# Two gate units moved between the steps of a state-space scan, and their sigmoids behind it

## The reference

```
proj = h @ w_in[i]
q, k, v, z, xbc, dt_raw, gates = split_cols(proj, IN_SPLITS)
...
attn_out = gqa_attention(q, k, v) @ w_attn_proj[i]
ssd_y = ssd_branch(z, xbc, dt_raw, ...)
ssd_out = ssd_y @ w_ssd_proj[i]
g_attn, g_ssd = jnp.split(jax.nn.sigmoid(gates), N_BRANCH, axis=-1)
mixed = (g_attn * attn_out + g_ssd * ssd_out) @ w_out[i]
...
def ssd_chunked(xs, dt, a, bm, cm):
    y_diag = jnp.einsum("bcgls,bcgrls,bcsgrp->bclgrp", cb, decay_in, xd)
    states = jnp.einsum("bclgn,bcgrl,bclgrp->bcgrpn", bc, decay_states, xd)
    def step(h, inp):
        st, dec = inp
        return h * dec[..., None, None] + st, h
    _, prev = lax.scan(step, h0, (states, chunk_decay))
    y_off = jnp.einsum("bclgn,bcgrpn,bcgrl->bclgrp", cc, prev, jnp.exp(a_cs))
    return y_diag + y_off
```

## Time and profile before

| | us |
|---|---|
| median of 3 runs | 2368.75 |
| lowest, highest | 2365.58, 2369.27 |
| the profiled execution | 2360.32 |
| its span, first to last instruction | 2358.5 |

### The profile page before, as it was taken

One profiled execution on the slowest core, in us unless ns is written; L12 is line 12 of the kernel. 1 busy time (PEld: TensorE's weight loads), 2 busy tenths in 40 slices (PEclk: granted clock), 3 DMA queues, 4 the chain that ended last, 5 costly groups with the idle time before them and its releaser, 6 DMA issues.

```text
span 2358.5 us, 28203 instructions
## 1 busy us (share of the span) xinstructions
PE 2202.5 (93%) x10837; PEld 1825.0 (77%) x10848; DVE 1143.1 (48%) x1836; ACT 1007.5 (43%) x2029; POOL 959.9 (41%) x730
## 2 busy tenths in 40 slices
PE   7999899999988997899999997897899999999997
PEld 6788778888877776778888876775597887888886
DVE  3445565554345666465553364564535335544322
ACT  5666444443235564254442256455344234323222
POOL 3555554343456752453443433123423334322232
PEclk9999999999989999899999998898999999999998
DMA  4112122322213221123223211110012221232221
GB/s 156 54 54 72 51 93 90 107 90 99 98 61 110 81 68 34 60 72 106 91 94 109 92 65 36 37 37 19 19 46 91 97 107 72 90 106 91 101 98 52
DMA packets 29846, 183.08 MB, mean 78 GB/s; under 512 B 3984, under 2 KB 4112, under 8 KB 11920
## 3 DMA queue, kind: packets, MB, share of 16 engines
q1 hardware_dynamic: 29712, 181.27, 22.2%
HBM read 174.97 MB, written 2.10 MB: 75 GB/s over the span
## 4 chain that ended last, share of the span: by engine, by line
PE 82%; DVE 7%; ACT 5%; issue 3%; POOL 2%; DMA 0%; SPq 0%; POOLq 0%; ACTq 0%; DVEq 0%
PE PS L1423 80%; PE PS L1548 1%; POOL LO L2702 1%; DVE bQS L2160 1%; DVE cCVT L2585 0%; PE PS L1661 0%; DMA RAW<-wall 0%; ACT HI L1750 0%; DVE aQS L2160 0%; POOL bTQ L2760 0%; DVE cST L2566 0%; POOL bROT L2755 0%; DVE YH L2262 0%; DVE XL L2237 0%; DVE T_f L2232 0%
## 5 line engine op out<-in xcount | busy, mean ns | idle before, releaser
L2702 POOL TENSOR_TENSOR LO<-RAW,HI 128x512 fp32r<-128x512 f32 (+2 forms) x382 | 540.7, 1432 | 623.9 <-ACT HI L1750 623.6
L1423 PE MATMUL PS<-XH,HI 128*128 128x512 f32 (+1 forms) x1584 | 640.4, 404 | 34.1 <-ACT cCU L2067 10.4
L1423 PE MATMUL PS<-XH,LO 128*128 128x512 f32 (+1 forms) x1584 | 626.0, 395 | 0.0
L1423 PE MATMUL PS<-XL,HI 128*128 128x512 f32 (+1 forms) x1584 | 619.7, 396 | 1.4 <-DVE XL L2237 1.4
L1750 ACT ACTIVATE HI<-RAW 128x512 fp32r<-128x512 f32 (+3 forms) x668 | 365.7, 608 | 171.3 <-PE PS L1423 168.0
L2160 DVE TENSOR_TENSOR LO<-RAW,HI 128x512 fp32r<-128x512 f32 (+2 forms) x286 | 304.5, 1069 | 248.3 <-ACT HI L1750 248.0
L1423 PEld LDWEIGHTS PS<-XH,HI 128*128 128x128 f32 (+1 forms) x1584 | 302.9, 191 | 98.0 <-issue 21.0
L1423 PEld LDWEIGHTS PS<-XH,LO 128*128 128x128 f32 (+1 forms) x1584 | 302.1, 191 | 66.0 <-issue 1.1
L1423 PEld LDWEIGHTS PS<-XL,HI 128*128 128x128 f32 (+1 forms) x1584 | 301.7, 191 | 63.9 <-DVE XL L2237 3.3
L1423 PE MATMUL PS<-HH,HI 128*128 128x512 f32 x528 | 205.4, 389 | 0.0
L1423 PE MATMUL PS<-HL,HI 128*128 128x512 f32 x528 | 205.4, 389 | 0.0
(11 more groups left out here) (397 smaller groups left out, 3355.7 us busy)
## 6 DMA issues: line engine op xcount, KB each, us to landing
RAW<-wall SPq DMA_DIRECT2D x138, 1024.0 KB, 4.8
RAW<-wall SPq DMA_DIRECT2D x24, 896.0 KB, 4.4
bROT<-bTQ SPq DMA_DIRECT2D x64, 64.0 KB, 2.0
RAW<-wall SPq DMA_DIRECT2D x5, 512.0 KB, 3.3
XF<-xT SPq DMA_DIRECT2D x4, 512.0 KB, 5.3
outT<-XR SPq DMA_DIRECT2D x8, 256.0 KB, 2.0
FP<-cfp SPq DMA_DIRECT2D x1, 1024.0 KB, 6.8
MKF<-cmask SPq DMA_DIRECT2D x1, 704.0 KB, 11.0
```

Of the source, the lines that this page charges most:

```text
L1423: return e.matmul(out, a, b, start=start, stop=stop)
L2702: return e.tensor_tensor(out, x, h.bitcast(F32), ALU.subtract)
```

## The change

The two gate units of quarter 0, `cga` 0 and `cgs` 0, are taken between the last `cx` unit and the first `cz` unit. `opening()` and `scans()` are chained into one generator that runs beside their 32 k-steps at 1.6 steps each, together with what is left of the chores; the `cz` units get the old rate of 0.36. The evacuation of a gate tile becomes a step of its own, `mgp`. The scaled products of quarter 0 wait in a new tile `GA0` and in `CTH`, and their four sigmoids stand behind `yn`; quarter 0 mixes in `CU` in place of `SG`. The heads keep banks 2 and 3, the states take bank 4 + g for both directions, since the gate tiles need banks 0 and 1. In `scans` each state step now ends with a `yield`. In the mix, the order for quarter 0 becomes `cpa` 0, `cga` 1, the eight `yt`, `cps` 0; quarter 1 begins with `cpa` 1.

```
-RATES = (0.37, 0.18, 1.0, 0.36, 1.0, 0.9, 0.9)
+RATES = (0.37, 0.18, 1.0, 1.6, 1.0, 0.9, 0.9, 0.36)
...
+    out += [("cq", 0), ("ck", 0), ("cq", 1), ("cv", 0)] + [("cx", j // 2) for j in CONV[::2]] + [("cga", 0), ("cgs", 0)]
+    out += [("cz", i) for i in range(4)] + [("cpa", 0), ("cga", 1), ("cps", 0)]
+    for i in range(1, 4):
+        out += [("cga", i)] * (i > 1) + [("cpa", i), ("cgs", i), ("cps", i)]
...
-                    at_bank(("sh", h, dr), 2 + dr + 2 * (h % 2))
+                    at_bank(("sh", h, dr), 2 + dr)
...
-                        b, s = pick(), ("so", dr, idx, g)
+                        b, s = 4 + g, ("so", dr, idx, g)
...
-                        b, s = pick(), ("sp", dr, idx, g)
+                        b, s = 4 + g, ("sp", dr, idx, g)
...
                 for i in range(PACE):
-                    next(left[(PACE * n + i) % 2], None)
+                    if next(left[(PACE * n + i) % 2], finished) is not finished:
+                        yield
...
-        first = opening()
-        while chores or together_chores:
-            chore()
-            next(first, None)
-        for _ in first:
-            pass
-        alongside(scans(), RATES[3])
+        def gate(kind, i, later=False):
+            for j, t in enumerate(lin_fm((kind, i), "X", evac=lambda j, t: product(kind, i, j, t))):
+                if not later:
+                    put("m" + kind[1:], i, j)
+
+        def product(kind, i, j, t):
+            freed[tiles[t].bank] = ("mgr", put("mgp", "m" + kind[1:], i, j, t))
+
+        alongside(itertools.chain(opening(), scans()), RATES[3])
+        gate("cga", 0, True)
+        gate("cgs", 0, True)
         until(lambda: sdone[0] >= 4 and all(finished))
+        beside[1] = RATES[7]
...
+        for kind in ("mga", "mgs"):
+            for j in range(2):
+                put(kind, 0, j)
+        shares(0)
+        gate("cga", 1)
         for j in range(8):
             b, s = pick(), ("yt", j)
...
+        mix(0)
+        for i in range(1, 4):
+            if i > 1:
+                gate("cga", i)
+            shares(i)
+            gate("cgs", i)
+            mix(i)
...
+    GA0 = sb("cGA0", 1024, F32, E0 + 32 * K)
...
+            return blk(GA0 if kind == "mga" else CTH, j)
...
-            elif kind in ("mga", "mgs"):
-                i, j, t = a
-                x = 1024 * j + (512 if kind == "mgs" else 0)
+            elif kind == "mgp":
+                gk, i, j, t = a
                 e.wait_ge(*when_(ag.tiles[t].full))
-                if i > 0:
+                if i > 1:
                     e.wait_ge(*when("mxl", *whole["mps", i - 1, j]))
-                e.tensor_tensor(SG[:, x:x + 512], PS[ag.tiles[t].bank][:, :], RPS[:, :], ALU.mult).then_inc(SEM["mgr"], 1)
+                elif i == 0 and gk == "mgs":
+                    e.wait_ge(*when("cxm", "cxm", CONV[-1]))
+                elif i == 0:
+                    e.wait_ge(*when("turn", "tu", 3))
+                e.tensor_tensor(gated(gk, i, j), PS[ag.tiles[t].bank][:, :], RPS[:, :], ALU.mult).then_inc(SEM["mgr"], 1)
```

53 lines of the change are left out of this document (25 added, 28 removed).

## The result

The changed kernel takes 2378.54 us (median of 5 runs, 2375.28 to 2384.01), the kernel before 2365.58 in the same comparison; the ratio is 1.0056, with a 95% interval from 1.0041 to 1.0071. It is slower by about 13 us. The forecast was +7.5 us, 2376.3, in a range of 2365 to 2385; it started from 2368.75, the median of three runs that was known then.

What follows compares the result with a forecast made beforehand. TensorE, busy for 93% of the span, was taken as the bound, so time could come only from its waits or half clock. Scan +13.2 and mix -5.7 gave +7.5 on 2368.75, so 2376.3 us, range 2365.0 to 2385.0.

Steps and rivals of the forecast that it cites:

- the forecast's own case: Whole kernel: slower by +4.7 to +12 us, around the +7.5 forecast; chance 0.45.
- The mix: From last `cz` matmul to `cpa` 1: gives back only 5.7 us, with new waits of 7.3 and 8.9 us.
- The scan: Scan with both gates moved in: 84.4 us instead of 71.2, +13.2, as 15.4 us stay above 69.0 of work.
- the start: Scan's beginning: TensorE at half clock until 1620, 3.4 us lost (bounds 1.5 and 6).
- the bursts: Two state runs `sp so so sp so so` in the scan: waits on VectorE's chain, 7.0 us together (bounds 5.0 and 8.5).
- the copy on ScalarE behind the eight `y0`: Scan: backward `sp` shares the forward one's bank and waits for this copy, 1.8 us (bounds 0 and 3).
- small waits: Scan's opening and between states: 0.2, 0.6, 0.5 and 0.3, in sum 1.6 us; last `cxt` among them.
- falls of the clock: Scan: one fall to half clock after a wait, 1.6 us (bounds 0 and four falls, 6.4).
- The new banks: Scan: heads on two banks and states sharing one per group, priced as waits at some 3 us.
- The clock's rule: Skill page: only a long idle gap costs the clock; by it the change comes out 1.6 us better; not followed.
- The fast one: Rival: the clock holds and waits shrink, scan +5.4, mix gives 10.5, together -5.1, 2363.7 us; chance 0.08.
- The convoy: Rival: gate steps and scan steps delay each other, ScalarE may bound, nothing hidden, +16.1, 2384.9 us; chance 0.17.

Runs made afterwards that it cites:

- e1_cover: Changed kernel with the mix reordered: `cga` 1 ahead of `cpa` 0 and `cgs` 1 ahead of `cps` 0, scan untouched; 2362.43 us, ratio 0.9990 to the kernel before.
- e11_defer: e7_toggle with one more convolution piece issued per opening piece, the last convolution's transposition `cxt` 7 kept at its old place on TensorE; 2357.56 us.
- e2_block: Changed kernel with both gate units in one block behind the scan instead of between its steps; 2398.7 us, ratio 1.0144 to the kernel before.
- e3_banks: Kernel before with only the new banks, heads on 2 and 3, states on 4 + g, no gate moved; ratio 1.0090, runs 2372.49 to 2393.27 us.
- e5_states: Kernel before with only a state's product put in the bank of its group, heads keeping four banks, no gate moved; 2386.07 us, ratio 1.0071.
- e6_heads: Kernel before with only the heads put on banks 2 and 3, states in turn as before, no gate moved; 2367.19 us, ratio 1.0002.
- e7_toggle: e1_cover with the states' products and outputs taking banks 4 and 5 in turn instead of by group; 2361.64 us, ratio 0.9979 to the kernel before.
- e12_gaps2: e11_defer with late gate k-steps put into the bursts' waits, one kept between the last head's broadcasts and its output; 2353.56 us, ratio 0.9946 to before.

## Why the prediction was right or wrong

- **The sign and the range.** Right: slower, +13 where +7.5 was forecast; 2378.5 lies within 2365 to 2385. It lies above the forecast's own case (+4.7 to +12) by 1 us. That 2378.5 is only 2 us from 2376.3 is in part luck: the forecast was added to 2368.75, and the kernel before took 2365.58 in the comparison. The change was 5.5 us larger than forecast.
- **The `cz` stretch, nothing.** Right: 74.1 against 74.0.
- **The mix, -5.7.** Right: -6.6, and by the mechanism named. The wait ahead of `cga` 1 was 6.8 (7.3 forecast), `cps` 0 ran step by step, and `cpa` 1 stood 51 us behind the last `cz`. The parts were off and made up for each other: the waits are 12.3 and not 16.2, the clock's loss 8.7 (7.3 without what falls into the long wait) and not 4.8. A chain that VectorE and ScalarE pace ends when it ends, and slow matmuls within it only fill its waits. e1_cover shows that this loss of cover is worth 16 us.
- **The scan, +13.2.** Mis-sized by 6: +19.2. Term by term, forecast and measured: the start 3.4 and 3.4; the bursts 7.0 and 7.1; the copy on ScalarE behind the eight `y0` 1.8 and nothing (it ended at 1658.79 and the product that needs it stands at 1658.84, after gate k-steps at half clock, which covered it); small waits 1.6 and 4.4, of which `cxt` 7 alone has 3.8 where I wrote 0.5, and the last head's output 0.6 where I wrote nothing; falls of the clock 1.6 and about 4.7, one of which, 2.6, is the fall behind `cxt` 7; and 1.8 without a name. So the step that failed is the last `cxt` in the list of small waits. I followed TensorE's list, costed VectorE and ScalarE by their free shares, and did not walk their queues: on ScalarE the convolution's first piece stands behind exponentials and `y0`, and on VectorE its other pieces stand behind a head's product that waits for ScalarE. e11_defer takes away the wait, and some 3 to 4 us with it.
- **The hidden part.** I said that 8.6 of the 21.8 us would be hidden; against the kernel before it was 2.6. The scan of 90.4 also passes my own mark, over 90, at which the gates were to hide nothing. Yet they do much: against the same banks without them in the scan they save 20 us (e2_block). I thought of cover for waits, and the waits stayed at 11.5; what they gave was clock, 8.1 lost instead of 13.5.
- **"The gates keep TensorE denser, so I take one fall."** The number was wrong (two large falls), the thought was right and larger than I made it: with the same banks and no gates the kernel takes 2391 (e3_banks, though one of its four runs took 2372), with the gates' work in a block 2399 (e2_block), and with the gates between the steps 2379.
- **The new banks.** I priced them at some 3 us, as waits. Without gates the states' pairing costs 6 to 24 (e5_states) and the heads' two banks nothing (e6_heads). With the gates in place, going back to banks in turn gives 1 to 3, which the intervals don't tell from nothing (e7_toggle), so in the changed kernel the price was not far off, by luck: the k-steps cover it.
- **The clock's rule.** After 0.87, 2.09 and 0.87 of waits in one burst four matmuls take 3.46 instead of 1.95. The Trainium skill, "TensorE: Matmul & The Clock Gate", section "HAM oscillation — how this bites in real kernels", has only a long gap cost the clock; the trace disagrees here as it did before.
- **The rivals.** The fast one is out: half clock at the start lasted 7.6 us and the mix lost its clock. The convoy (+16.1) came nearer than I allowed, to within 3 us. Its own mark was over 20 us of waits and half clock: what stands above the 69.0 of work is 21.4, of which 19.6 have a name. Of its place I had half. ScalarE, which I named, was late with the first piece of the last convolution, but it was not the bound behind it: there VectorE's queue was, and ScalarE stood idle for 4.18 ahead of the piece that it makes near the end:

```profile
1650.69 0.63 ACT L2106 ACTIVATE cCTH<-cCVT 128x512 f32<-128x512 f32 x1 [4.18 <-DVE cCVT L2609]
```

What stays open: why the clock comes back in one execution of e3_banks and e5_states and not in another, which part of e11_defer's gain is ScalarE's order and which VectorE's, which part of e12_gaps2's last 4 us is the last head's wait, and whether the first wait of 0.69 alone keeps the clock down in the kernels with paired banks.

## What to carry to other kernels

When work is moved out of a stretch, first look at what it covered there: here the two gates hid the chain of Y's scaling and the evacuation of `yt`, and two units put back in such places gave 16 us, more than the later edits of the scan together (9). When work is moved into a stretch, walk the queue of each engine in order at every place where TensorE takes something from it, since a free share of over 30% did not help a piece that stood behind a waiting one. Where the clock can fall, count what the added work does to it beside what it fills: here it filled as many waits as it made, and gained by the clock. Check that a short idle in a profile is not a missing record. Put filler into the waits themselves, and judge a version by its many runs: a profile's stretches tell where time goes, not how much a version gains.

## What the runs showed of the hardware

- Unchanged code took up to 13.7 us more or less until the scan (1606.96 to 1620.63 for the same matmul). One stretch in it, behind the same wait of 2.13, took 8.9 us in before and 10.5 in after, as the clock held there or not.
- Behind a wait of 0.69 us that the kernel before does not have, TensorE stayed at half clock for some 31 us in e3_banks (1619.9 to 1651, with further waits of 2.84 and 0.69 in it), and the scan had 0.60 as a mean in e5_states; in before the clock was back at 1622.5, within 4 us of the same place. With gate k-steps there, the same sharing of banks cost nothing that the intervals tell.
- The same 32 k-steps of gate work cost 20 us less between the scan's steps than in a block behind them, at nearly the same idle time of TensorE (14.8 and 15.5 us) and a mean clock of 0.91 instead of 0.68.
- An operation of VectorE on two operands in SBUF took 1.76 and 1.78 instead of 0.69 to 0.74 when it began while GpSimd was inside an operation of its own; one that began ahead of GpSimd's and overlapped it took 0.68.
